# Input and forget gates of a two-way mLSTM mixer: from columns per token to rows along time

## Chip, cores and metric

One Trainium2 chip, one of its cores. The metric is device time of one execution in microseconds (us). The engines named are TensorE (PE, with PEld its weight loads), VectorE (DVE), ScalarE (ACT), GpSimd (POOL) and SyncE (SP), which issues the weight transfers.

## The reference, cut to what matters

Two blocks follow each other on 256 tokens of width 1024 in float32: first a gated DeltaNet layer and an attention layer with feed-forward halves, then a block with adaptive modulation, feed-forward halves and a token mixer. The change is in that mixer. It projects 256 context tokens and 256 latent tokens and runs a stabilised mLSTM over each, forward and backward, with 4 heads of 256. The context run starts from zero and gives the state from which the latent run starts. Its gates are 16 of the projected columns: for each direction an input gate and a forget gate for each of 4 heads.

```python
gate_pre = (gates[0], jax.nn.log_sigmoid(gates[1]), gates[2], jax.nn.log_sigmoid(gates[3]))
# one direction, one chunk; lix: input gates, lfx: log forget gates, along time
b = jnp.cumsum(lfx, axis=-1)
dmat = b[..., :, None] - b[..., None, :] + lix[..., None, :]
inter = b + m[..., None]
m_t = jnp.maximum(inter, jnp.max(jnp.where(lower, dmat, -jnp.inf), axis=-1))
w, a = jnp.exp(dmat - m_t[..., None]), jnp.exp(inter - m_t)
h = num / jnp.maximum(jnp.abs(den), jnp.exp(-m_t))[..., None]
```

So the kernel needs, for 8 pairs of direction and head, a running sum of softplus(-f) along time, a running maximum of (input gate + sum), and exponentials of these, partly as rows along time and partly as columns, one value for each token.

## The kernel before, in words

Nearly all the work is matrix products with weights that stream from HBM in chunks of 1 MB. Each chunk is cut into a high and a low part (`whi` by ACT, line 382; `wlo` by DVE, line 388), and each product is three float32r products: high by high, high by low, low by high. Chunks go through rings of three buffers. `cut_ahead(engine, c)` stands in ACT's and DVE's order after the work on chunk c and cuts chunk c+3; ACT's cut waits until the products of chunk c are done (`used`), DVE's until ACT's is done, the products of a chunk wait for DVE's, and a later transfer into the raw buffer waits for DVE's as well. The order of work on each engine is written out by hand at the end of the file; engines meet by semaphores, and each runs its own list strictly in order.

The stretch around the change runs over segments of the weight stream: `down3` (end of a feed-forward half), `c_k`, `c_v` (context keys and values), `l_k`, `l_v`, `l_q` (latent keys, values, queries), `l_f`, `l_o`. `c_k`, `l_k`, `l_q` have 4 chunks each, with 48 products of 256 moving columns per chunk (line 411, for the first chunk of `l_k` line 472); `c_v`, `l_v` have 4 chunks with 24 products of 512 columns (line 454). `stream_pe(..., more)` calls `more(j)` after the products of chunk j. `conv_act` copies a chunk's result out of PSUM with a bias (`tap_x`, line 1983), applies Silu to the chunk before (line 1975), cuts ahead and then does its own `more(j)`; `conv_dve` does three-tap convolutions (lines 2004 to 2012), cuts ahead and calls `more(j)`. `values_dve` takes the values out of PSUM.

The gates pass (`gates_pe`, products recorded at line 411 on tiles `swh`, `swl`) uses activations as the stationary operand and 16 weight columns as the moving one: 2 token tiles x 8 x 3 = 48 products of 16 columns, once for the context before `c_k` and once for the latent after chunk 1 of `l_k`. `m_gates_dve` and `m_gates_act` form softplus(-f) on columns. `m_rows_pe` (lines 2077 to 2091) makes rows and running sums out of the columns by products with the identity, with all ones and with triangles; `m_rows_dve` copies the rows out and scans for the maximum; `m_rows_act` takes exponentials; `m_cols_pe` (line 2149) turns rows back to columns by products with a 4x4 identity. Then `st_pe` (line 2258) multiplies queries and keys, `cm_pe` (2242, 2244) spreads rows over partitions, `part_pe` forms the outputs. `update_pe`, `update_act`, `update_dve` (lines 2195, 2207, 2214) build the 8 context states: ACT scales keys to `kw`, PE multiplies, DVE copies out. `turn_*` transposes the next input, `rms_*` normalises it: ACT squares, POOL takes the root (line 1932), DVE scales (line 1937). `load_params` issues small parameter transfers on SP's queue between the first weight chunks, ahead of the transfer of `table`, for which `params_pe` waits.

Of the kernel before, what the change touches and what calls it, by code (L numbers as in the profile page):

```python
# [23 lines left out]
P = 128  # L24
# [30 lines left out]
    "m_gate": ("clev0", 4), "m_soft": ("w_ps", 24), "m_log": ("wlev", 24),  # L55
    "m_exp": ("twt_ps", 24), "m_rows_ps": ("invup", 20), "m_rows": ("invtup", 24),
    "m_first": ("row_am", 4), "m_next": ("decl", 16), "m_scan": ("deca", 16), "m_nlast": ("erow", 2),
# [31 lines left out]
def shape_tables():  # L89
# [18 lines left out]
    for h in range(4):  # L108
        sel[h, h] = 1
# [35 lines left out]
def build(nc, A, out):  # L145
# [351 lines left out]
    gate_bias = sm(16)  # L497
# [37 lines left out]
    def load_params(act):  # L535
        for g, members in enumerate(groups):
# [5 lines left out]
        act.dma_start(gate_bias, A["b_in_2"][:, COL_GATES:COL_BR].broadcast_to([P, 16]))\  # L542
           .then_inc(S("params_in"), 16)
        act.dma_start(table[:, P:N_TABLE], A["table"][:, P:N_TABLE]).then_inc(S("tables_in"), 16)
    N_PARAM_DMA = sum(len(m) for m in groups) + 3
# [306 lines left out]
    def small_weight_cut(dve, n):  # L852
        dve.wait_ge(*S("gates_in", 16 * (n + 1)))
        dve.tensor_copy(swh[:, :, :], g_raw[:, :, :]).then_inc(S("gates_cut"), 1)
        dve.wait_ge(*S("gates_cut", 2 * n + 1))
# [3 lines left out]
    def gates_pe(pe, n, out_bank):  # L859


        pe.wait_ge(*S("gates_cut", min(2 * n + 2, 4)))
        if n == 1:
            pe.wait_ge(*S("gate_row", 4))
        for tt in range(TT):
# [5 lines left out]
            last = products(pe, ps[out_bank][:, 16 * tt:16 * tt + 16], pairs)  # L871
# [5 lines left out]
    def gdn_in_pe(pe):  # L877
        pe.wait_ge(*S("act_lo", 4))

        def more(j):  # L880
            if j == 0:
                params_pe(pe)
                gates_pe(pe, 0, 7)
# [1056 lines left out]
    def ffn_banks(tt, h):  # L1940
# [19 lines left out]
    m_state, m_zero, m_nlast = sm(2), sm(2), sm(2)  # L1960
    m_wkc = sm(16).rearrange("p (d t h) -> p d t h", d=2, t=2)
    m_col = sm(48).rearrange("p (d t c h) -> p d t c h", d=2, t=2, c=3)
# [72 lines left out]
    def m_gates_dve(dve, n):  # L2035

        dve.wait_ge(*S("gates_ps", n + 2))
        flat_g = m_gate.rearrange("p t d c h -> p t (d c h)")
# [834 lines left out]
```

## Time and profile before

| | us |
|---|---|
| median of 3 runs | 1801.19 |
| lowest, highest | 1796.42, 1809.6 |
| profiled execution: its own time | 1805.2 |
| its span in the trace | 1803.4 |
| PE busy / DVE / ACT / POOL | 1712.1 / 970.0 / 764.5 / 221.4 |

The span runs from the first to the last instruction of the trace; 1.8 us of the execution's time lie around it. Positions below are us from the span's start. Matrix products are pipelined and their ends are modelled, so the distance from start to start tells their cost. A float32 product (not float32r) shows as two records. The mean granted clock of TensorE over the execution is 0.973 of 2.4 GHz.

### The profile page before, as it was taken

The page shows a single profiled execution, that of the slowest core. Times are in us where ns is not written, and L with a number is a line of the kernel's source. Part 1 is how long each engine was busy: PE and PEld are TensorE (multiplying, and loading weights), DVE is VectorE, ACT ScalarE, POOL GpSimd, SP SyncE. Part 2 cuts the span into 40 slices and gives each one's busy share as a digit, 9 for nine tenths or more (in the row PEclk, how much of TensorE's full clock was granted, in tenths as well). Part 3 has the DMA queues.
Part 4 walks back from the last instruction along what each step waited for, and adds up shares of the span by engine and source line. Part 5 has one row for each costly group of instructions (what it writes and reads, how often), then busy time and mean ns, then how long its engine had stood idle before and what let it go on. Part 6 is the DMA issues. An engine that isn't in the chain of part 4 may idle for free. (4 is left out here: it accounts for less than half of the span.)

```text
span 1803.4 us, 27891 instructions
## 1 busy us (share of the span) xinstructions
PE 1712.1 (95%) x12010; PEld 1567.6 (87%) x12010; DVE 970.0 (54%) x1076; ACT 764.5 (42%) x971; POOL 221.4 (12%) x185
## 2 busy tenths in 40 slices
PE   7999998999897889999999999999999999979998
PEld 7996888998684678988999899989899999969996
DVE  4663247554744464556755565555656354755543
ACT  4453433443344334433444354435455344444442
POOL 0123414000300040001400030002000020030000
PEclk8999999999898999999999999999989899989999
DMA  7554257665467577656765666554434224556652
GB/s 223 164 165 140 71 164 213 184 187 187 163 214 271 169 232 220 181 192 203 189 176 187 187 187 175 177 187 152 133 124 150 74 82 141 167 137 183 171 190 89
DMA packets 329281, 306.56 MB, mean 170 GB/s; under 512 B 12066, under 2 KB 287047, under 8 KB 329031
## 3 DMA queue, kind: packets, MB, share of 16 engines
q1 hardware_dynamic: 324358, 296.20, 53.4%
q10 hardware_dynamic: 4528, 7.54, 1.2%
q8 instruction: 95, 1.56, 0.4%
q0 software_dynamic: 272, 1.05, 0.2%
q14 instruction: 28, 0.22, 0.0%
HBM read 303.70 MB, written 1.05 MB: 169 GB/s over the span
## 5 line engine op out<-in xcount | busy, mean ns | idle before, releaser
L388 DVE TENSOR_TENSOR wlo<-raw,whi 128x2048 fp32r<-128x2048 f32 x247 | 583.7, 2366 | 392.7 <-ACT whi L382 392.5
L411 PE MATMUL ps<-ah,whi 128*128 128x256 f32 x2368 | 679.3, 287 | 7.4 <-DVE wlo L388 7.4
L411 PE MATMUL ps<-al,whi 128*128 128x256 f32 x2368 | 673.2, 284 | 0.0
L411 PE MATMUL ps<-ah,wlo 128*128 128x256 f32 x2368 | 673.0, 284 | 0.0
L382 ACT CAST whi<-raw 128x2048 fp32r<-128x2048 f32 x247 | 469.9, 1904 | 227.4 <-PE ps L435 157.1
L411 PEld LDWEIGHTS ps<-ah,whi 128*128 128x128 f32 x2368 | 457.9, 193 | 12.5 <-issue 9.0
L411 PEld LDWEIGHTS ps<-al,whi 128*128 128x128 f32 x2368 | 457.8, 193 | 1.8 <-issue 1.4
L411 PEld LDWEIGHTS ps<-ah,wlo 128*128 128x128 f32 x2368 | 457.6, 193 | 0.0
L756 ACT ACTIVATE f_sig<-ps 128x256 f32<-128x256 f32 x110 | 42.1, 383 | 372.4 <-PE ps L411 355.9
L435 PE MATMUL ps<-whi,fh 128*128 128x512 f32 x440 | 171.5, 390 | 0.0
L435 PE MATMUL ps<-wlo,fh 128*128 128x512 f32 x440 | 171.2, 389 | 0.0
L435 PE MATMUL ps<-whi,fl 128*128 128x512 f32 x440 | 171.2, 389 | 0.0
L785 DVE TENSOR_TENSOR f_act<-ps,f_sig 128x256 f32<-128x256 f32 x110 | 46.5, 423 | 153.0 <-ACT f_sig L756 152.9
L454 PE MATMUL ps<-whi,ah 128*128 128x512 f32 x256 | 103.1, 403 | 3.1 <-DVE al L616 1.8
L454 PE MATMUL ps<-wlo,ah 128*128 128x512 f32 x256 | 100.9, 394 | 0.0
L454 PE MATMUL ps<-whi,al 128*128 128x512 f32 x256 | 100.7, 393 | 0.0
L435 PEld LDWEIGHTS ps<-whi,fl 128*128 128x128 f32 x440 | 82.6, 188 | 17.1
L435 PEld LDWEIGHTS ps<-wlo,fh 128*128 128x128 f32 x440 | 82.6, 188 | 16.9
L435 PEld LDWEIGHTS ps<-whi,fh 128*128 128x128 f32 x440 | 82.6, 188 | 16.9
L454 PEld LDWEIGHTS ps<-whi,ah 128*128 128x128 f32 x256 | 49.0, 191 | 14.2 <-issue 2.6
L454 PEld LDWEIGHTS ps<-whi,al 128*128 128x128 f32 x256 | 48.8, 191 | 10.5
L454 PEld LDWEIGHTS ps<-wlo,ah 128*128 128x128 f32 x256 | 48.9, 191 | 10.0 <-issue 0.2
(359 smaller groups left out, 1778.0 us busy)
## 6 DMA issues: line engine op xcount, KB each, us to landing
raw<-in_f_w SPq DMA_DIRECT2D x132, 512.0 KB, 4.6
raw<-in_w_a SPq DMA_DIRECT2D x132, 512.0 KB, 4.5
raw<-in_w_ada SPq DMA_DIRECT2D x72, 512.0 KB, 4.6
raw<-in_w_in SPq DMA_DIRECT2D x68, 512.0 KB, 4.6
raw<-in_w_b SPq DMA_DIRECT2D x66, 512.0 KB, 4.5
raw<-in_a_w_in SPq DMA_DIRECT2D x32, 512.0 KB, 5.2
raw<-in_b_w_qkv SPq DMA_DIRECT2D x24, 512.0 KB, 4.8
raw<-in_a_w_out SPq DMA_DIRECT2D x8, 512.0 KB, 3.9
```

What stands on the lines that cost most here:

```text
L382: act.copy(whi[:, c % RING, :], raw[:, r % RING, :]).then_inc(S("hi_ready"), 1)
L388: dve.tensor_tensor(wlo[:, c % RING, :], raw[:, r % RING, :], whi[:, c % RING, :].bitcast(F32), ALU.subtract).then_inc(S("lo_ready"), 1)
L411: last = pe.matmul(out_ap, a, b, start=(i == 0), stop=(i == n - 1))
L435: last = pe.matmul(ps[4 + 2 * tt + h][:, :], x[:, k, cols_], y[:, kk, n], start=(k == 0 and i == 0), stop=(k == KF - 1 and i == 2))
L454: last = pe.matmul(ps[q.bank[first + tt]][:, :], x[:, 4 * half + kk, cols_], y[:, kk, :], start=(half == 0 and kk == 0 and i == 0), stop=( ...
L756: act.activation(f_sig[:, j % RING, :], ps[b][:, 0:T], ACT.Silu).then_inc(S("silu"), 1)
L785: dve.tensor_tensor(f_act[:, j % RING, :], ps[b][:, T:2 * T], f_sig[:, j % RING, :], ALU.mult)\
```

## The change

The gate weights are spread over 100 of 128 stationary columns: POOL zeroes two tiles `gwh`, `gwl` (`gate_weights_pool`), DVE cuts the 16 weight columns into them (`gate_weights_dve`) so that forward and backward input gates fall on rows 0 to 3 and 32 to 35 of the result and forget gates on rows 64 to 67 and 96 to 99. The weights become the stationary operand and the activations the moving one: 8 x 3 = 24 products of 256 columns give rows along time at once (`m_gates_pe`), for the context after chunk 1 of `c_k`, for the latent after chunk 1 of `l_k`. ACT takes them out of PSUM with a bias for each row (`m_gates_act`), DVE forms |f| (`m_size_dve`), ACT applies Exp and Ln one chunk later (`m_soft_act`, each with its table load), DVE forms the running sums by scans and then the running maxima (`m_rows_dve`, one chunk later again). `m_rows_pe` is gone. `m_cols_pe` turns 36 rows at once: 2 products in place of 4 for the context, 6 in place of 12 for the latent, the latter moved from after `l_f` chunk 0 to after `l_q` chunk 1. `m_cols_dve` copies in 2 and 6 instructions in place of 1 and 1. The bias is now loaded by four transfers in place of one, after two DVE memsets, and `sel` holds ones on rows 32 to 35 too.

```diff
+        for d in range(2):
+            for c in range(2):
+                row, at_ = 64 * c + 32 * d, COL_GATES + 8 * d + 4 * c
+                act.dma_start(gate_bias[row:row + 4, :],
+                              A["b_in_2"][0, at_:at_ + 4].rearrange("(h o) -> h o", o=1))\
+                   .then_inc(S("params_in"), 16)
         act.dma_start(table[:, P:N_TABLE], A["table"][:, P:N_TABLE]).then_inc(S("tables_in"), 16)
-    N_PARAM_DMA = sum(len(m) for m in groups) + 3
+    N_PARAM_DMA = sum(len(m) for m in groups) + 6
+    def setup_dve(dve):
+        dve.memset(gate_bias[0:64, :], 0.0).then_inc(S("bias_zero"), 1)
...
     cell = at("cell", 47.125, [P, 2, NH, 2, W1])
-    m_r0, m_cm0, m_a, m_r1, m_s1, m_cm1 = (at(f"m_row{kb}_{i}", kb, [P, 2, T])
-                                           for i, kb in enumerate((74, 76, 39.125, 72, 74, 76)))
+    gwh, gwl = at("gwh", 25.125, [P, KD, P], F32R), at("gwl", 29.125, [P, KD, P], F32R)
+    m_sp, m_s, m_r, m_cm = ([at(f"m_row{n}{kb}", kb, [P, T]) for n, kb in enumerate(kbs)]
+                            for kbs in ((74, 72), (75, 73), (76, 74), (77, 76)))
+    m_a = at("m_a", 77, [P, T])
     w_buf = [at(f"w_buf{kb}", kb, [P, 512]) for kb in (8, 10, 12, 14, 72, 74)]
     m_nq = at("m_nq", 63.25, [P, NH, W1])
-    m_gate = sm(32).rearrange("p (t d c h) -> p t d c h", t=2, d=2, c=2)
-    m_sp, m_mx = (sm(16).rearrange("p (t d h) -> p t d h", t=2, d=2) for _ in range(2))
...
+    def gate_weights_pool(pool):
+        pool.wait_ge(*used("down3", segs["down3"].n - 1))
+        pool.memset(gwh[:, :, :].bitcast(F32), 0.0).then_inc(S("gw_zero"), 1)
+        pool.memset(gwl[:, :, :].bitcast(F32), 0.0).then_inc(S("gw_zero"), 1)
+    def gate_weights_dve(dve):
+        dve.wait_ge(*S("gates_in", 32))
+        dve.wait_ge(*S("gw_zero", 2))
+        w = g_raw[:, :, :].rearrange("p k (d c h) -> p k d c h", d=2, c=2)
+        hi, lo = (g[:, :, :].rearrange("p k (c d r) -> p k d c r", c=2, d=2) for g in (gwh, gwl))
+        for c in range(2):
+            dve.tensor_copy(hi[:, :, :, c, 0:4], w[:, :, :, c, :]).then_inc(S("m_gw"), 1)
+        for c in range(2):
+            dve.wait_ge(*S("m_gw", c + 1))
+            dve.tensor_tensor(lo[:, :, :, c, 0:4], w[:, :, :, c, :], hi[:, :, :, c, 0:4].bitcast(F32), ALU.subtract)\
+               .then_inc(S("m_gw"), 1)
+    def m_gates_pe(pe, n):
+        pe.wait_ge(*S("m_gw", 4))
+        if n == 0:
+            pe.wait_ge(*S("gate_row", 4))
+        pairs = []
+        for k in range(KD):
+            pairs += [(gwh[:, k, 0:100], ah[:, k, :]), (gwh[:, k, 0:100], al[:, k, :]), (gwl[:, k, 0:100], ah[:, k, :])]
+        products(pe, ps[3][0:100, 0:T], pairs).then_inc(S("gates_ps"), 1)
+    def m_gates_act(act, n):
+        act.wait_ge(*S("gates_ps", n + 2))
+        act.activation(m_sp[n][ROWS, :], ps[3][64:100, 0:T], ACT.Identity, bias=gate_bias[64:100, :])\
+           .then_inc(S("m_f"), 1)
+        act.activation(m_r[n][ROWS, :], ps[3][ROWS, 0:T], ACT.Identity, bias=gate_bias[ROWS, :])\
+           .then_inc(S("m_f"), 1)
+    def m_size_dve(dve, n):
+        f, least = m_sp[n][ROWS, :], m_s[n][ROWS, :]
+        dve.wait_ge(*S("m_f", 2 * n + 2))
+        dve.tensor_scalar(least, f, 0.0, None, ALU.min).then_inc(S("m_soft"), 1)
+        dve.wait_ge(*S("m_soft", 3 * n + 1))
+        dve.scalar_tensor_tensor(f, least, -2.0, f, ALU.mult, ALU.add).then_inc(S("m_soft"), 1)
+    def m_soft_act(act, n):
+        f = m_sp[n][ROWS, :]
+        act.wait_ge(*S("m_soft", 3 * n + 2))
+        act.activation(f, f, ACT.Exp, scale=-1.0).then_inc(S("m_exp"), 1)
+        act.wait_ge(*S("m_exp", n + 1))
+        act.activation(f, f, ACT.Ln, bias=1.0).then_inc(S("m_log"), 1)
+    def along(buf, d):
+        a = buf[DIRS[d], :]
+        return a[:, ::-1] if d else a
+    def m_rows_dve(dve, n):
+        sp, cum, r, cm = m_sp[n], m_s[n], m_r[n], m_cm[n]
+        if n == 0:
+            for buf in (m_zero, m_nlast, m_state):
+                dve.memset(buf[ROWS, :], 0.0).then_inc(S("m_zeros"), 1)
         dve.wait_ge(*S("m_log", n + 1))
-        dve.tensor_tensor(m_sp, m_sp, m_mx, ALU.add).then_inc(S("m_soft"), 1)
...
+        dve.tensor_tensor(sp[ROWS, :], sp[ROWS, :], cum[ROWS, :], ALU.subtract).then_inc(S("m_soft"), 1)
+        dve.wait_ge(*S("m_soft", 3 * n + 3))
+        dve.wait_ge(*S("m_zeros", 3))
         for d in range(2):
-            u = tab("uf" if d == 0 else "ub")
...
+            dve.tensor_tensor_scan(along(cum, d), along(sp, d), along(sp, d), m_zero[DIRS[d], :], ALU.add, ALU.max)\
+               .then_inc(S("m_cum"), 1)
+        dve.wait_ge(*S("m_cum", 2 * n + 2))
+        dve.tensor_tensor(r[ROWS, :], r[ROWS, :], cum[ROWS, :], ALU.add).then_inc(S("m_r"), 1)
+        dve.wait_ge(*S("m_r", n + 1))
+        if n:
+            dve.wait_ge(*S("m_next", 2))
         for d in range(2):
-            u = tab("uf" if d == 0 else "ub")
...
+            init = (m_zero, m_state)[n]
+            dve.tensor_tensor_scan(along(cm, d), along(r, d), along(r, d), init[DIRS[d], :], ALU.max, ALU.max)\
+               .then_inc(S("m_scan"), 1)
         dve.wait_ge(*S("m_scan", 2 * n + 2))
         if n == 0:
             for d in range(2):
-                last = cm[0:4, d, (T - 1, 0)[d]:(T, 1)[d]]
-                dve.tensor_scalar(m_nlast[0:4, d:d + 1], last, -1.0, None, ALU.mult).then_inc(S("m_nlast"), 1)
-                dve.tensor_tensor(m_state[0:4, d:d + 1], last, ps[5][0:4, d:d + 1], ALU.subtract)\
-                   .then_inc(S("m_next"), 1)
+                p, t = slice(32 * d, 32 * d + 4), slice((T - 1, 0)[d], (T, 1)[d])
+                dve.tensor_scalar(m_nlast[p, :], cm[p, t], -1.0, None, ALU.mult).then_inc(S("m_nlast"), 1)
+                dve.tensor_tensor(m_state[p, :], cm[p, t], cum[p, t], ALU.subtract).then_inc(S("m_next"), 1)
         else:
-            dve.tensor_tensor(m_s1[0:4, :, :], m_cm1[0:4, :, :], m_s1[0:4, :, :], ALU.subtract)\
-               .then_inc(S("m_mt"), 1)
+            dve.tensor_tensor(cum[ROWS, :], cm[ROWS, :], cum[ROWS, :], ALU.subtract).then_inc(S("m_mt"), 1)
     def m_rows_act(act, n):
         if n == 0:
             act.wait_ge(*S("m_nlast", 2))
-            for d in range(2):
-                act.activation(row(m_r0, d), row(m_r0, d), ACT.Exp, bias=m_nlast[0:4, d:d + 1])\
-                   .then_inc(S("m_wk"), 1)
+            act.activation(m_r[0][ROWS, :], m_r[0][ROWS, :], ACT.Exp, bias=m_nlast[ROWS, :]).then_inc(S("m_wk"), 1)
             return
         act.wait_ge(*S("m_scan", 4))
-        for d in range(2):
-            act.activation(row(m_a, d), row(m_cm1, d), ACT.Exp, scale=-1.0, bias=m_state[0:4, d:d + 1])\
-               .then_inc(S("m_a"), 1)
+        act.activation(m_a[ROWS, :], m_cm[1][ROWS, :], ACT.Exp, scale=-1.0, bias=m_state[ROWS, :])\
+           .then_inc(S("m_a"), 1)
         act.wait_ge(*S("m_mt", 1))
-        act.activation(m_s1[0:4, :, :], m_s1[0:4, :, :], ACT.Exp, scale=-1.0).then_inc(S("m_em"), 1)
+        act.activation(m_s[1][ROWS, :], m_s[1][ROWS, :], ACT.Exp, scale=-1.0).then_inc(S("m_em"), 1)
     def m_cols_pe(pe, n):
         if n == 0:
-            pe.wait_ge(*S("m_wk", 2))
-            out_, kinds = ps[4], [m_r0]
+            pe.wait_ge(*S("m_wk", 1))
+            pe.wait_ge(*S("res_scaled", 8))
+            kinds = [m_r[0]]
         else:
-            pe.wait_ge(*S("m_a", 2))
+            pe.wait_ge(*S("m_a", 1))
             pe.wait_ge(*S("m_em", 1))
-            pe.wait_ge(*evicted("l_q", 3))
-            out_, kinds = ps[1], [m_r1, m_a, m_s1]
-        for d in range(2):
+            pe.wait_ge(*S("cell", 16))
+            kinds = [m_r[1], m_a, m_s[1]]
+        for c, buf in enumerate(kinds):
             for tt in range(TT):
-                for c, buf in enumerate(kinds):
-                    at_ = ((d * 2 + tt) * len(kinds) + c) * 4
-                    last = pe.matmul(out_[:, at_:at_ + 4], buf[0:4, d, tt * P:tt * P + P], ident[0:4, 0:4],
-                                     start=True, stop=True)
+                at_ = 36 * (TT * c + tt)
+                last = pe.matmul(ps[4][:, at_:at_ + 36], buf[ROWS, tt * P:tt * P + P], ident[ROWS, 0:36],
+                                 start=True, stop=True)
         last.then_inc(S("m_cols_ps"), 1)
     def m_cols_dve(dve, n):
         dve.wait_ge(*S("m_cols_ps", n + 1))
-        if n == 0:
...
+        for c in range((1, 3)[n]):
+            dst = m_wkc if n == 0 else m_col[:, c, :, :, :]
+            for d in range(2):
+                src = ps[4][:, 72 * c:72 * c + 72].rearrange("p (t r) -> p t r", t=TT)[:, :, 32 * d:32 * d + 4]
+                dve.tensor_copy(dst[:, :, d, :], src).then_inc(S("m_cols"), 1)
     def k_tok_pe(pe, blocks):
         for b in blocks:
...
@@ -2555,13 +2559,10 @@
         pe.wait_ge(*S("act_lo", 24))
         ffn_pe(pe, 3, gate=1, down_turn=6)
         pe.wait_ge(*S("act_lo", 28))
-        gates_pe(pe, 1, 3)
-        stream_pe(pe, "c_k", ah, al)
-        pe.wait_ge(*S("m_gate", 1))
+        stream_pe(pe, "c_k", ah, al, lambda j: m_gates_pe(pe, 0) if j == 1 else None)
+        pe.wait_ge(*S("m_f", 2))
         def context_rows(j):
-            if j == 0:
-                m_rows_pe(pe, 0)
             if j == 2:
                 m_cols_pe(pe, 0)
                 k_tok_pe(pe, (0, 1))
...
         def keys_and_gates(j):
             if j == 1:
-                gates_pe(pe, 2, 3)
+                m_gates_pe(pe, 1)
             updates({0: 2, 1: 3, 3: 4})(j)
         stream_pe(pe, "l_k", ah, al, keys_and_gates, turn=7)
-        pe.wait_ge(*S("m_gate", 2))
+        pe.wait_ge(*S("m_f", 4))
         stream_pe(pe, "l_v", ah, al, updates({0: 5, 1: 6, 2: 7}))
-        stream_pe(pe, "l_q", ah, al, lambda j: m_rows_pe(pe, 1) if j == 0 else None)
+        stream_pe(pe, "l_q", ah, al, lambda j: m_cols_pe(pe, 1) if j == 1 else None)
         stream_pe(pe, "l_f", ah, al, only=[0])
-        m_cols_pe(pe, 1)
...
         res_act(act, segs["down3"])
-        m_gates_act(act, 0)
-        conv_act(act, "c_k", kt, lambda j: rms_act(act, 3, x0, "res", 3) if j == 2 else None)
+        def context_gates(j):
+            if j == 1:
+                m_gates_act(act, 0)
+            if j == 2:
+                m_soft_act(act, 0)
+                rms_act(act, 3, x0, "res", 3)
+        conv_act(act, "c_k", kt, context_gates)
         q = segs["c_v"]
...
             if j == 1:
                 m_gates_act(act, 1)
             else:
+                if j == 2:
+                    m_soft_act(act, 1)
                 update_act(act, {0: 3, 2: 4, 3: 5}[j])
         conv_act(act, "l_k", kt, keys_and_gates)
...
-        conv_act(act, "l_q", qt, lambda j: m_rows_act(act, 1) if j == 2 else None)
+        conv_act(act, "l_q", qt, lambda j: m_rows_act(act, 1) if j == 0 else None)
...
         res_dve(dve, 0)
         ffn_dve(dve, 3, up_work=lambda e, j: rms_dve(e, 2, x1) if j == UP_AT else None, down_work=lambda e: turn_dve(e, 6, mod_scale(1)))
-        m_gates_dve(dve, 0)
+        gate_weights_dve(dve)
         mask_dve(dve)
         res_dve(dve, 1)
-        conv_dve(dve, "c_k", lambda j: rms_dve(dve, 3, x0) if j == 2 else None)
+        def context_gates_dve(j):
+            if j == 1:
+                m_size_dve(dve, 0)
+            if j == 2:
+                rms_dve(dve, 3, x0)
+            if j == 3:
+                m_rows_dve(dve, 0)
+        conv_dve(dve, "c_k", context_gates_dve)
         def context_rows_dve(j):
-            if j == 0:
...
         def cells_and_gates(j):
             if j == 1:
-                m_gates_dve(dve, 1)
+                m_size_dve(dve, 1)
             if j:
                 update_dve(dve, j + 1)
+            if j == 3:
+                m_rows_dve(dve, 1)
         conv_dve(dve, "l_k", cells_and_gates)
         values_dve(dve, "l_v", lambda j: update_dve(dve, 5 + j) if j < 3 else None)
-        conv_dve(dve, "l_q", lambda j: m_rows_dve(dve, 1) if j == 1 else None)
+        conv_dve(dve, "l_q", lambda j: m_cols_dve(dve, 1) if j == 2 else None)
...
         gate_rows_pool(pool, 1)
         rms_pool(pool, 2)
         turn_pool(pool, 6, mod_shift(1))
+        gate_weights_pool(pool)
         res_pool(pool, 1, x0)
```

## Rows read from the trace of the kernel before

**Rows 1.** Page, busy time of each engine, share of the span, instructions.

```profile
PE 1712.1 (95%) x12010; PEld 1567.6 (87%) x12010; DVE 970.0 (54%) x1076; ACT 764.5 (42%) x971; POOL 221.4 (12%) x185
```

**Rows 2.** Waits of PE from 1185 to 1440: total, times, longest.

```profile
PE ps L472 <- DVE al L616: 1.9, 1, 1.9
```

**Rows 3.** Timeline of PE, context gates and `c_k`: start, duration, instruction.

```profile
1227.64 0.17 PE L411 MATMUL ps<-swh,ah 128*128 128x16 f32 x1
...
1234.56 0.56 PE L411 MATMUL ps<-ah,whi 128*128 128x256 f32 x1
...
1238.05 0.28 PE L411 MATMUL ps<-al,whi 128*128 128x256 f32 x1
```

**Rows 4.** Timeline of PE, latent gates, updates and chunk 2 of `l_k`.

```profile
1307.19 0.17 PE L411 MATMUL ps<-swh,ah 128*128 128x16 f32 x1
...
1315.07 3.77 PE L2195 MATMUL ps<-v_aug,kw 128*128 128x257 f32 x8
1318.28 0.78 PE L411 MATMUL ps<-ah,whi 128*128 128x256 f32 x1
...
1319.91 0.28 PE L411 MATMUL ps<-ah,whi 128*128 128x256 f32 x1
...
1324.94 0.28 PE L411 MATMUL ps<-ah,whi 128*128 128x256 f32 x1
...
1330.70 1.89 PE L2195 MATMUL ps<-v_aug,kw 128*128 128x257 f32 x8
1332.24 0.58 PE L454 MATMUL ps<-whi,ah 128*128 128x512 f32 x1
```

**Rows 5.** Windows: length, busy PE, PEld, DVE, ACT, POOL, granted clock, DMA.

```profile
1232.00:1234.00 2.00, 2.00 (x11) 2.00 (x11) 0.12 (x1) 1.39 (x3) 1.66 (x6) 0.50 0.38 52
```

**Rows 6.** Timeline of PE, first instruction of each rows pass and its successor.

```profile
1264.71 0.38 PE L2077 MATMUL ps<-table,small 128*4 128x128 f32 x2
...
1267.16 0.50 PE L454 MATMUL ps<-whi,ah 128*128 128x512 f32 x1
...
1365.37 0.38 PE L2077 MATMUL ps<-table,small 128*4 128x128 f32 x2
...
1368.95 0.39 PE L411 MATMUL ps<-ah,whi 128*128 128x256 f32 x1
```

**Rows 7.** Timeline of PE, latent columns and the two query-key passes with their successors.

```profile
1392.17 0.38 PE L2149 MATMUL ps<-table,m_row 4*128 4x4 f32 x2
...
1394.94 5.46 PE L2258 MATMUL ps<-qt,kt 128*128 128x128 f32 x32
1400.15 0.48 PE L2242 MATMUL ps<-negr,identr 128*128 128x512 f32 x1
...
1422.34 3.74 PE L2258 MATMUL ps<-qt,kt 128*128 128x128 f32 x32
1425.83 0.48 PE L2242 MATMUL ps<-negr,identr 128*128 128x512 f32 x1
```

**Rows 8.** Timeline of ACT: update after `l_k` chunk 3; a switch to Exp.

```profile
1333.95 0.91 ACT L2207 ACTIVATE kw<-k_tok,small 128x256 f32<-128x256 f32 x2
...
1382.01 1.90 ACT L382 CAST whi<-raw 128x2048 fp32r<-128x2048 f32 x1
1383.93 1.28 ACT L2131 ACT_TABLE_LOAD   x1
1385.22 0.91 ACT L2131 ACTIVATE m_row39.125_2_94<-m_row,small 4x256 f32<-4x256 f32 x2
```

**Rows 9.** Timeline of DVE, chunks 2 and 3 of `c_k`; what it waited for in brackets.

```profile
1259.88 0.75 DVE L1937 TENSOR_SCALAR xn<-x,small 128x1024 f32<-128x1024 f32 x1 [0.72 <-POOL small L1932]
...
1264.25 2.28 DVE L388 TENSOR_TENSOR wlo<-raw,whi 128x2048 fp32r<-128x2048 f32 x1
```

**Rows 10.** All scans on the row tiles: duration in ns, minimum, median, maximum.

```profile
L2110 DVE TENSOR_TENSOR_SCAN m_row<-m_row,small x4: 712/724/737, 1269.9 to 1382.4; 4x256 f32<-4x256 f32 x4
```

**Rows 11.** Timeline of SP's queue, issue of the one bias transfer.

```profile
16.31 0.43 SPq L542 DMA_DIRECT2D small<-in_b_in  x1
```

More of the change, by code:

```diff
@@ L108, in shape_tables @@
     for h in range(4):
-        sel[h, h] = 1
+        sel[h, h] = sel[32 + h, h] = 1
     t["sel"] = sel.reshape(P, 4 * P)
@@ L870, in gates_pe @@
                           (al[:, k, c], swh[:, k, :])]
-            last = products(pe, ps[out_bank][:, 16 * tt:16 * tt + 16], pairs)
+            last = products(pe, ps[7][:, 16 * tt:16 * tt + 16], pairs)
         last.then_inc(S("gates_ps"), 1)
@@ L882, in more @@
                 params_pe(pe)
-                gates_pe(pe, 0, 7)
+                gates_pe(pe)
             if j == 2:
@@ L2051, in m_gates_act @@
-    def m_gates_act(act, n):
-        act.wait_ge(*S("m_soft", 4 * n + 3))
-        act.activation(m_sp, m_sp, ACT.Exp, scale=-1.0).then_inc(S("m_exp"), 1)
-        act.wait_ge(*S("m_exp", n + 1))
-        act.activation(m_sp, m_sp, ACT.Ln, bias=1.0).then_inc(S("m_log"), 1)
-    def front(d):
-        return d
-    def row(buf, d):
-        return buf[0:4, d, :]
-    def m_rows_pe(pe, n):
-        pe.wait_ge(*S("m_soft", 4 * n + 4))
-        if n == 0:
-            pe.wait_ge(*S("res_scaled", 8))
-        else:
-            pe.wait_ge(*S("cell", 16))
-        for d in range(2):
-            u = tab("uf" if d == 0 else "ub")
-            for tt in range(TT):
-                o = ps[4][0:4, T * d + P * tt:T * d + P * tt + P]
-                pe.matmul(o, m_gate[:, tt, d, 0, :], ident, start=(d == tt == 0), stop=False)
-                if tt != front(d):
-                    pe.matmul(o, m_sp[:, front(d), d, :], ones, start=False, stop=False)
-                pe.matmul(o, m_sp[:, tt, d, :], u, start=False, stop=(d == tt == 1))
-        for d in range(2):
-            u = tab("uf" if d == 0 else "ub")
-            for tt in range(TT):
-                if n == 0:
-                    last = pe.matmul(ps[5][0:4, d:d + 1], m_sp[:, tt, d, :], ones[:, 0:1],
-                                     start=(tt == 0), stop=(tt == 1))
-                else:
-                    o = ps[5][0:4, T * d + P * tt:T * d + P * tt + P]
-                    if tt != front(d):
-                        pe.matmul(o, m_sp[:, front(d), d, :], ones, start=(d == tt == 0), stop=False)
-                    last = pe.matmul(o, m_sp[:, tt, d, :], u, start=(d == tt == 0), stop=(d == tt == 1))
-        last.then_inc(S("m_rows_ps"), 1)
@@ L2094, in m_rows_dve @@
[L2094 to L2110 removed]
+    ROWS = slice(0, 36)
@@ L2243, in cm_pe @@
             for h in range(NH):
-                last = pe.matmul(bank(b, NH)[:, h, :], tab("sel", 4)[0:4, h, :], m_cm1[0:4, d, tile],
+                last = pe.matmul(bank(b, NH)[:, h, :], tab("sel", 4)[32 * d:32 * d + 4, h, :], m_cm[1][32 * d:32 * d + 4, tile],
                                  start=(i == 2 and h == 0), stop=(h == NH - 1))
@@ L2311, in part_act @@
             wait_from(act, *S("hout", i - 3))
-            act.activation(m_nq[:, h, :], ps[part_banks(h)[0]][:, 0:W1], ACT.Copy, scale=m_col[:, d, t, 1, h:h + 1])\
+            act.activation(m_nq[:, h, :], ps[part_banks(h)[0]][:, 0:W1], ACT.Copy, scale=m_col[:, 1, t, d, h:h + 1])\
                .then_inc(S("nq"), 1)
@@ L2726, in _ @@
     def _(dve):
+        setup_dve(dve)
         turn_dve(dve, 0)
         start_cuts(dve)
-        small_weight_cut(dve, 0)
+        small_weight_cut(dve)
         gdn_in_dve(dve)
```

86 lines of the change are left out of this document (23 added, 63 removed).

## The prediction

> **What bounds the kernel now.** I read the page's busy times first [rows 1]: PE is busy 95% of the span, no other engine over 54%. The share says little about one stage, so next come the waits of PE in the stretch that the change touches: in 255 us there is one wait, of 1.9 us [rows 2], before the transposed input of `l_k`, and it follows PE's own transposes. So in this stretch PE's list is the critical path, and every us that leaves PE's list or its starts comes off the time, unless ACT or DVE fall behind. The third view is the timeline of PE, read start to start, because recorded durations overlap. In the fast state a product of 256 columns costs (1324.94 - 1319.91) / 42 = 0.120 us [rows 4], a chunk of 48 such products 5.76 us. The fourth is the windows: in the middle of the first gates pass the granted clock is 0.50, the lower of TensorE's levels (1.2 GHz), though PE sat idle nowhere [rows 5]. What PE did before the fall was products of 16 columns, and it stayed at the low level into the chunk behind them.
>
> **Parts that leave or change PE's list.**
>
> (a) Context gates. From the first product of the pass to the first of `c_k` it is 1234.56 - 1227.64 = 6.92 us [rows 3]. The next 16 products take 1238.05 - 1234.56 = 3.49 us, 0.218 each, against 16 x 0.120 = 1.92: a tail of 1.57. In their place come 24 products of 256 columns: 2.88 us at 0.120, at most 5.2 at the slow 0.218. The nearest row is the stream's own product, the same form but for 28 stationary columns, so I take 2.88. Gain 6.92 + 1.57 - 2.88 = 5.61.
>
> (b) Latent gates. 1315.07 - 1307.19 = 7.88 us for the pass. The update behind it takes 1318.28 - 1315.07 = 3.21, where an ordinary one takes 1332.24 - 1330.70 = 1.54: 1.67 more. Six slow products take 1.63 instead of 0.72, of which I leave 0.2 to the handover: 0.7 more [rows 4]. Gain 7.88 + 1.67 + 0.7 - 2.88 = 7.37.
>
> (c) The products for rows go: 1267.16 - 1264.71 = 2.45 for the context, 1368.95 - 1365.37 = 3.58 for the latent [rows 6]. Gain 6.03.
>
> (d) Products for columns. The latent pass takes 1394.94 - 1392.17 = 2.77 us for 24 records, 0.115 each [rows 7]. Six float32 products leave 12 records, 1.38 us, among full chunks of `l_q`; for the context 4 records of 8 go, 0.46. Gain 1.39 + 0.46 = 1.85. A 36-row product could cost up to the 0.163 of a slow query-key record (5.21 / 32, below); that is 0.8 us less for the 16, and nothing makes it cheaper than 0.115.
>
> (e) The query-key pass that followed those columns products takes 1400.15 - 1394.94 = 5.21 us, the second one, with the same records and no columns products ahead of it, 1425.83 - 1422.34 = 3.49 [rows 7]. With the small products gone from its front I expect 3.49. Gain 1.72, bounds 0 and 3.2 (a later slow stretch might go too, or the same one move behind it).
>
> Gross: 5.61 + 7.37 + 6.03 + 1.85 + 1.72 = 22.6 us.
>
> Of the first two and the last, 1.57 + 1.67 + 0.7 + 1.72 = 5.7 us are the slow clock's and not the products'. The Trainium skill, in "TensorE: Matmul & The Clock Gate", section "HAM oscillation", puts the fall down to idle gaps of the array. By that rule PE, which has no idle gap here, would not owe its slow stretches to these products, and they would stay. The rows show the fall without a gap, so I hold to the rows; the rule's outcome is the first rival.
>
> **Parts that other engines now owe PE.**
>
> (f) ACT before the update after `l_k` chunk 3. PE finishes chunk 3 at 1330.70 and ACT starts that chunk's own extra work at 1333.95 [rows 4, 8]: 3.25 us for copying out, Silu and the cut. In the new order chunk 2's extra work is Exp and Ln on 256 columns, each behind a table switch, and then the two `kw` for update 4. A switch takes 1.28, an activation of 256 columns 0.91 / 2 = 0.45 to 0.5 [rows 8]: 2 x 1.28 + 2 x 0.5 = 3.6 us. If PE ends chunk 2 at X, the first `kw` is there at X + 3.25 + 3.6 + 0.45 = X + 7.3; PE wants it after chunk 3, at X + 5.76. A new stall of 1.55 us, 1.6 with the handover. Queued behind on ACT is the copy of chunk 3 out of its bank, which `l_v` needs: it ends 0.5 before that.
>
> The rows show no more than the load itself: cut until 1383.91, load at 1383.93, Exp at 1385.22 [rows 8]. The Trainium skill, "ScalarE: Activation LUTs", section "What ACT_TABLE_LOAD costs", adds a drain of about 1.38 us to each. By it the stall would be 1.6 + 2.8 = 4.4 and the sum below 17.4 instead of 20.2; the rows decide.
>
> (g) DVE's cuts for `c_v`. Before, chunk 2 of `c_k` ended at 1238.05 + 128 x 0.120 = 1253.4; DVE's first scaling of the next input, which needs ACT's squares and POOL's root, began at 1259.88, 6.5 later, and the list from there to the cut took 4.37 and the cut 2.28 [rows 3, 9]. Now chunk 2 ends at 1227.64 + 3 x 5.76 + 2.88 = 1247.8, and (f)'s 3.6 us stand ahead of the squares: 1247.8 + 6.5 + 3.6 + 4.37 + 2.28 = 1264.5. PE wants this chunk after four of `c_k` (1253.56) and two of `c_v`, of (1264.71 - 1253.4 - 5.76) = 5.5 each [rows 3, 6]: 1264.6. Just met. Then DVE runs the new rows block: four scans at 0.72 [rows 10] are 2.9, two whole-tile steps and seven small ones some 1.4 (my estimate from half a scan each for the former), 4.3 in all; bounds 2.5 and 7, since an adding scan has no row of its own. The cut behind it is done at 1264.5 + 4.3 + 2.3 = 1271.1. PE wants it after a third chunk (1270.1), the columns products (0.46) and the key transposes behind them, so at 1270.6 or later. I put 0.1 us of stall; by the upper bound it is 2.7.
>
> (h) Start. Three more transfers are issued on SP ahead of `table` and of the fourth weight chunk; one takes 0.43 and a gap of 0.04 [rows 11], 1.4 in all. `params_pe` waits for `table`, the whole queue stands behind. Bounds 0 (table lands while chunk 0 is multiplied) and 1.4; I take 0.7.
>
> Covered, and therefore nothing: POOL's zeroing and DVE's cutting of the gate weights come 11 us before their first product, and the cut queued behind them on DVE serves a chunk three places on; should that cover go, DVE's delay shows there one for one. ACT's Exps for the latent columns, now behind `l_q` chunk 0 (end Y): 3.25 less a Silu of 0.5, then 1.28 + 2 x 0.5 ends at Y + 5.0, and PE asks at Y + 5.76, so 0.7 us of cover. The latent rows block stands behind the cut for `l_v` chunk 2 and ahead of the one for chunk 3, which PE needs three chunks and three updates later. Six column copies on DVE lie beside chunks 2 and 3 of `l_q`. After the stretch PE's waits follow PE's own transposes, so the shift should travel to the end.
>
> Net: 22.6 - 1.6 - 0.1 - 0.7 = 20.2 us. The profiled execution took 1805.2 us, 1.8 more than its span: 1785.0. It lay 4.0 above the median of three, so I forecast 1801.2 - 20.2 = 1781.0.
>
> **Rivals.**
>
> 1. The slow clock stays. For it: nothing here shows 100-column weights at work, and the low level needs no idle gap. Against: streams of 256-column products keep the high level all through. Then the 5.7 us stay and 48 products cost 0.218: 4.7 more. 20.2 - 10.4 = 9.8: 1791. Chance 0.12.
> 2. ACT and DVE fall behind. (g) has no slack, (f) is a stall already, and each us on DVE's rows block or ACT's switches is passed on. For it: two switches in series in front of squares, POOL, DVE and a cut. Against: all else keeps 0.5 us or more. With the upper bound of (g), 2.7, that of (h), 1.4, and 3 more in (f): 20.2 - 2.6 - 0.7 - 3 = 13.9: 1787. Chance 0.20.
> 3. It doesn't do what it says for the whole: the gain is made by 1400 and given back at a later wait that doesn't follow PE. Nothing in the stretch shows one, but I have not followed every wait to 1803. 1801. Chance 0.06.
> 4. Slower. One mechanism: scans with addition, or on 36 partitions, run ten times slower than the row of 0.72. The context block holds four, 26 us more in front of a cut without cover; the latent block four, 26 less some 10 of cover. 20.2 - 26 - 16 gives 1823. It turns slower than before once a scan costs over some 4.5 us. The scans measured, one of each pair reversed in time, lie within 25 ns of each other, so 0.04.
>
> **How the numbers follow.** Forecast 0.58, rivals 0.12, 0.20, 0.06, 0.04. About 1% (18 us) is what a measurement of this kernel can tell from no change; three runs spread over 13 us. The forecast lies only 2 us beyond that bound; rivals 1 to 3 lie within it. So faster 0.58, same 0.38, slower 0.04. Range: downward all of (e)'s upper bound, no stalls in (f) to (h) and some of the spread of medians, 1781 - 1.5 - 2.4 - 4 = 1773; upward rivals 2 and 1, 1792. Rivals 3 and 4 stay out.
>
> **What would show it.** Right: PE's granted clock at 1.00 through both gates passes, 24 products in 2.9 us, no product for rows, a wait of PE for ACT's `kw` of 1.6 us after `l_k` chunk 3, the first query-key pass at 3.5 us. Wrong in (a), (b): clock at 0.50 behind the new products. Wrong in (g): PE waiting for `wlo` in `c_v`. Wrong in (f): a wait above 3 us. The prediction fails if ACT's new place delays more than one cut, or if a slow stretch appears that before did not have.

## The result and the profile after

The changed kernel takes 1781.2 us (median of 4 runs, 1780.0 to 1786.1), the kernel before 1804.1 beside it (4 runs, 1796.4 to 1809.6): ratio 0.988, 95% interval 0.984 to 0.993. A second series gave 1782.7 against 1805.1 and 0.988 again. That is 1.2% faster, 22 to 23 us where 20.2 were forecast; the forecast time, 1781.0, was met to 0.2 us by luck: the difference was forecast 2 to 3 us too small, and the median of before that it started from, 1801.2, lay 3 to 4 us below the 1804 to 1805 of more runs. The profiled execution took 1782.3, 1.9 more than its span.

The page of the changed kernel first, span and busy times, which answer to [rows 1]:

```profile
span 1780.4 us, 27662 instructions
PE 1689.6 (95%) x11886; PEld 1547.3 (87%) x11886; DVE 975.9 (55%) x1087; ACT 766.2 (43%) x973; POOL 222.4 (12%) x187
```

The span is 23.0 us shorter, PE is busy 22.5 us less, and DVE only 6 us more. PE's waits from 1160 to 1440, as in [rows 2]:

```profile
PE ps L472 <- DVE al L626: 1.9, 1, 1.9
PE ps L2199 <- ACT kw L2211: 1.4, 1, 1.4
```

The old wait is there, and one new one, (f)'s. Timeline of PE: the context gates from their first to their last record and the stream's product behind them (against [rows 3]); the first record of the latent gates and the update behind them; the update after chunk 3 of `l_k` (against [rows 4]); the latent columns (one of four records, and their successor); and both query-key passes with their successors (against [rows 7]):

```profile
1241.80 0.28 PE L411 MATMUL ps<-ah,gwh 128*100 128x256 f32 x1
...
1244.49 0.28 PE L411 MATMUL ps<-ah,gwl 128*100 128x256 f32 x1
1244.60 0.28 PE L411 MATMUL ps<-ah,whi 128*128 128x256 f32 x1
...
1301.06 0.28 PE L411 MATMUL ps<-ah,gwh 128*100 128x256 f32 x1
...
1303.86 1.90 PE L2199 MATMUL ps<-v_aug,kw 128*128 128x257 f32 x8
...
1318.70 1.97 PE L2199 MATMUL ps<-v_aug,kw 128*128 128x257 f32 x8 [1.44 <-ACT kw L2211]
...
1359.21 0.63 PE L2155 MATMUL ps<-table,m_row 36*128 36x36 f32 x4
...
1360.66 0.39 PE L411 MATMUL ps<-ah,whi 128*128 128x256 f32 x1
...
1378.02 3.74 PE L2262 MATMUL ps<-qt,kt 128*128 128x128 f32 x32
1381.52 0.48 PE L2246 MATMUL ps<-negr,identr 128*128 128x512 f32 x1
...
1403.69 3.74 PE L2262 MATMUL ps<-qt,kt 128*128 128x128 f32 x32
1407.18 0.48 PE L2246 MATMUL ps<-negr,identr 128*128 128x512 f32 x1
```

Read start to start: 24 gates products take 2.80 us, 0.117 each, both times; 12 records for columns 1.45; the first query-key pass 3.50 where it was 5.21. The windows (length, busy PE, granted clock, DMA) show the high level, 2.4 GHz, in the middle of both gates passes, where [rows 5] had 0.50:

```profile
1242.00:1244.00 2.00, 2.00 (x19) 1.00 0.00 0
1302.00:1304.00 2.00, 2.00 (x19) 1.00 0.80 309
```

What lay behind the one new wait, from ACT's timeline (against [rows 8]):

```profile
1314.71 1.28 ACT L2092 ACT_TABLE_LOAD   x1
1316.01 0.42 ACT L2092 ACTIVATE m_row<-m_row 36x256 f32<-36x256 f32 x1
1316.45 1.28 ACT L2094 ACT_TABLE_LOAD   x1
1317.74 0.42 ACT L2094 ACTIVATE m_row<-m_row 36x256 f32<-36x256 f32 x1
1318.06 0.89 ACT L2211 ACTIVATE kw<-k_tok,small 128x256 f32<-128x256 f32 x2
1318.86 0.81 ACT L1989 ACTIVATE tap_x<-ps,cols 128x256 f32<-128x256 f32 x2
```

The second load begins 0.44 after the first Exp began: nothing but the 1.28 of the load itself stands between two activations. And DVE's new rows block of the context, between the cuts for chunks 2 and 3 of `c_v` (against [rows 9, 10]):

```profile
1263.74 2.29 DVE L388 TENSOR_TENSOR wlo<-raw,whi 128x2048 fp32r<-128x2048 f32 x1
...
1266.47 1.51 DVE L2111 TENSOR_TENSOR_SCAN m_row<-m_row,small 32x256 f32<-32x256 f32 x2
1268.01 0.42 DVE L2114 TENSOR_TENSOR m_row<-m_row,m_row 36x256 f32<-36x256 f32 x1
1268.46 1.51 DVE L2120 TENSOR_TENSOR_SCAN m_row<-m_row,small 32x256 f32<-32x256 f32 x2
...
1270.49 2.29 DVE L388 TENSOR_TENSOR wlo<-raw,whi 128x2048 fp32r<-128x2048 f32 x1
```

The block takes 4.5 us, a scan 0.74 by its own record (1.51 for two), whether it adds or takes the maximum, and PE does not wait for the cut.

**The stretch in marks.** I cut PE's timeline at instructions that both kernels have: end of the FFN (A), first transpose for `l_k` (B), first query-key pass (C), its end (D), second pass, its end (E), first product of the stream behind the outputs that follow the second pass (F). A is a position, the other columns are lengths. Each kernel was profiled twice:

| | A | A to B | B to C | C to D | E to F |
|---|---|---|---|---|---|
| before | 1227.6 | 58.89 | 108.41 | 5.21 | 14.06 |
| before, second profile | 1229.1 | 60.49 | 108.34 | 5.22 | 10.75 |
| after | 1230.3 | 50.11 | 97.62 | 3.50 | 10.41 |
| after, second profile | 1227.6 | 50.10 | 97.62 | 3.49 | 13.71 |

B to C and C to D repeat within 0.1 us here, which points to the list of instructions; the variants below show that B to C can also grow by 1.5 by a slow stretch that comes and goes. A to B differs by 1.6 between the profiles of before. D to E, not in the table, is 25.7 in three of the four and 24.2 in the second profile of before. E to F differs by 3.3 between two profiles of the same kernel, in either kernel: the fall of the clock there comes and goes. Had I compared the first pair alone, I would have booked 3.65 us to the change that it did not bring.

### The profile page after: what moved, and what is told of

The parts are those of the page before. It is cut to its first block and busy times, and to the rows that moved or that the text cites. A ratio compares the mean times of both kernels' runs of the same rounds, so it can differ in the third digit from the quotient of the medians.

```text
span 1780.4 us, 27662 instructions
## 1 busy us (share of the span) xinstructions
PE 1689.6 (95%) x11886; PEld 1547.3 (87%) x11886; DVE 975.9 (55%) x1087; ACT 766.2 (43%) x973; POOL 222.4 (12%) x187
## 5 line engine op out<-in xcount | busy, mean ns | idle before, releaser
L454 PEld LDWEIGHTS ps<-whi,al 128*128 128x128 f32 x256 | 48.6, 190 | 10.4
```

The costliest lines, as they stand in the source:

```text
L454: last = pe.matmul(ps[q.bank[first + tt]][:, :], x[:, 4 * half + kk, cols_], y[:, kk, :], start=(half == 0 and kk == 0 and i == 0), stop=( ...
```

## The experiments

**1. Is it the clock, and is PE's list the path?** Two kernels answer this. The first is the kernel before, which keeps its 48 products of each gates pass, but each reads the 16 columns 16 times over, so that it has 256 (the output and the copy behind it are widened to match):

```diff
+            r = 16 if n else 1
+            hi, lo = (w.unsqueeze(2).to_broadcast([P, KD, r, 16]) for w in (swh[:, :, :], swl[:, :, :]))
...
-                pairs += [(ah[:, k, c], swh[:, k, :]), (ah[:, k, c], swl[:, k, :]),
-                          (al[:, k, c], swh[:, k, :])]
+                pairs += [(ah[:, k, c], hi[:, k]), (ah[:, k, c], lo[:, k]), (al[:, k, c], hi[:, k])]
...
```

> The kernel before, with one edit: in the context and latent gates passes the moving operand of each of the 48 products repeats its 16 columns 16 times, 256 columns in all; the sums read are the same. Theory (the low clock comes from the products of 16 columns, not from idle gaps): both passes run at the high level, 48 x 0.120 = 5.8 us each in place of 6.9 + 1.6 and of 7.9 + 1.7 + 0.7, so although PE does 16 times the columns the time falls by 2.7 + 4.5 = 7.2 us. Rival (the slow stretch belongs to the place and stays): 48 x 0.218 = 10.5 us each, 6 us slower than before. Rival (a product's cost is its columns alone): 5.8 against the 6.9 and 7.9 of the passes, but with the tails still there, 3.2 us faster.

In the second the changed kernel runs each new gates pass twice:

```diff
+        products(pe, ps[3][0:100, 0:T], pairs)
         products(pe, ps[3][0:100, 0:T], pairs).then_inc(S("gates_ps"), 1)
```

> The changed kernel with each of its two new gates passes done twice, 48 products of 256 columns in place of 24. Theory (PE's list is the time here, the new products keep the clock): 2 x 24 x 0.120 = 5.8 us more than the changed kernel, about 16 us less than before. Rival (other engines set the time of this stretch by now): under 2 us more. Rival (products with 100 stationary columns lower the clock once there are enough of them): over 10 us more.

The first took 1798.4 (10 runs) against 1804.5 (14), ratio 0.997, interval 0.995 to 0.999. Sixteen times the columns took less time: 6.1 us less between the medians where 7.2 were expected. Its PE timeline, first product of each pass and what follows it, and three windows:

```profile
1224.89 0.28 PE L411 MATMUL ps<-swh,ah 128*128 128x256 f32 x1
...
1230.74 0.28 PE L411 MATMUL ps<-ah,whi 128*128 128x256 f32 x1
...
1309.14 1.90 PE L2197 MATMUL ps<-v_aug,kw 128*128 128x257 f32 x8
```

```profile
1226.00:1228.00 2.00, 2.00 (x19) 1.00 1.03 391
1304.00:1306.00 2.00, 2.00 (x19) 1.00 0.87 299
1290.00:1292.00 2.00, 2.00 (x12) 0.50 0.00 0
```

The pass takes 5.85 instead of 6.92 and leaves no tail: A to B is 2.63 shorter than in the first profile of before, as expected (2.7), and 4.2 shorter than in the second, where the pass took 7.93. B to C is 2.95 shorter, not 4.5: a new stretch at 0.50 came up at 1290, behind the old 1.9 us wait, and cost 1.5. The second kernel took 1785.7 (5 runs, ratio to before 0.991, 0.988 to 0.994). Its last windows in the two passes:

```profile
1247.00:1249.00 2.00, 2.00 (x20) 1.00 0.10 14
1309.00:1311.00 2.00, 2.00 (x19) 1.00 0.00 0
```

A to B grew by 2.80, B to C by 2.79, and neither C to D nor E to F moved against the first profile of the changed kernel: each us on PE's list is a us of the time there, and 48 products of 100 stationary columns in a row hold the high level as well. Over the whole kernel the medians differ by less than these 5.6 us, by 3.0 to 4.5 against the two series of the changed kernel.

**2. Does the first query-key pass owe its 1.7 us to the columns products ahead of it?** The six new products were moved back to straight ahead of the pass, into bank 1:

```diff
-        stream_pe(pe, "l_q", ah, al, lambda j: m_cols_pe(pe, 1) if j == 1 else None)
+        stream_pe(pe, "l_q", ah, al)
         stream_pe(pe, "l_f", ah, al, only=[0])
+        m_cols_pe(pe, 1)
...
```

> The changed kernel with the latent columns products put back to their old place, between chunk 0 of l_f and the first query-key pass, with bank 1 as their target as before; still 12 records. To be read in the trace. Theory of the prediction's step (e) (small products ahead of the query-key pass bring the clock down in it): the first query-key pass takes about 5.2 us again in place of 3.5, and the slow stretch near the second pass comes back too. Rival (it was the chance of where the slow stretch fell): the pass stays at 3.5 us.

One run: 1788.7. The pass was slow (5.12), but it also had a gap of 4.1 us in front, since it waited for the columns' eviction, so the run can't tell the products from the gap. In the next kernel it waits for the context's columns alone:

```diff
-            pe.wait_ge(*S("m_cols", 8))
+            pe.wait_ge(*S("m_cols", 2))
```

> The changed kernel with the six products for columns moved back to where they stood, straight ahead of the first query-key pass, in a bank of their own, and the pass no longer waiting for their eviction: the idle gap of 4.1 us in the run before this one is gone, and the products alone are left. If it was the gap that brought the clock down there: pass 3.5, second pass with its decay products and the part behind it 3.5, 3.55, 6.86 as in the changed kernel, total within 1 us of it. If short products ahead of the pass do it (as the rows and columns did before): pass 5.1, some 1.6 us, and perhaps the second fall too (3.7 us).

And with 24 products of 4 moving columns instead of the six of 36:

```diff
+                for lo, hi in ((0, 36),) if n == 0 else ((0, 4), (32, 36)) * 2:
+                    last = pe.matmul(ps[(4, 1)[n]][:, at_ + lo:at_ + hi], buf[ROWS, tt * P:tt * P + P],
+                                     ident[ROWS, lo:hi], start=True, stop=True)
```

> The changed kernel with the products for columns straight ahead of the first query-key pass, as in the run without the gap, but 24 products of 4 moving columns in place of 6 of 36 (each twice; the last writes stand): as near as it can be to what stood there in the kernel before. The products cost 2.8 in place of about 1.4. If products of few columns ahead of the pass are what brought the clock down in the kernel before, the pass takes 5.1 instead of 3.6 here; if not, it stays 3.5 to 3.6 and the cause lies further ahead (the rows products and the slow stretches that they leave).

They took 1785.3 and 1791.8 (one run each). The query-key pass in PE's timeline, in the three kernels in this order, in the third with the first row of the products ahead of it:

```profile
1379.11 5.36 PE L2262 MATMUL ps<-qt,kt 128*128 128x128 f32 x32 [4.08 <-issue]
```

```profile
1377.29 3.84 PE L2262 MATMUL ps<-qt,kt 128*128 128x128 f32 x32
```

```profile
1373.58 1.95 PE L2156 MATMUL ps<-table,m_row 36*128 36x4 f32 x16
...
1379.33 6.75 PE L2263 MATMUL ps<-qt,kt 128*128 128x128 f32 x32
```

and the windows of the third, PE busy throughout:

```profile
1376.00:1378.00 2.00, 2.00 (x20) 1.00 1.02 356
1378.00:1380.00 2.00, 2.00 (x13) 0.66 0.20 30
1380.00:1382.00 2.00, 2.00 (x11) 0.50 0.97 263
```

So two different things bring the clock down: a gap (first kernel, 0.50 in its window behind it) and products of few columns without any gap (third kernel). Behind the six products of 36 columns, 1.45 us, the pass took 3.6 (second kernel). They cost PE the same as among `l_q`; B to C came out 1.4 longer by one stretch of low clock behind the 1.9 us wait. That bears out (e), with two reserves. The 24 products left 48 records and took 5.75 us, where [rows 7] had 24 records in 2.8, so the dose was larger than the original (the pass behind took 6.5, not 5.2). And each of the two kernels has one trace; but the pass took 5.2 in all three traces with the old columns products ahead of it (two of before, one of the widened kernel) and 3.5 in all seven that have the new ones among `l_q`.

**3. How much of it belongs to the list?** Both kernels profiled again, unaltered.

> The changed kernel once more, unaltered, as the bound for what one profile can say. If the fall of the clock behind the second query-key pass (3.7 us in the profile of the kernel before, none in that of the changed one) belongs to the instruction list, this profile has none either: second pass 3.49, its decay products 3.55, the part behind them 6.86. If it comes and goes from run to run, one of the three may be longer. The stretch from the end of the FFN to the first query-key pass stays 147.7 within 0.3. Ratio to before 0.988.

> The kernel before once more, unaltered, with a profile. If the slow first query-key pass (5.21) belongs to its instruction list, it is 5.2 again; if it comes and goes as the fall behind the second pass does in the changed kernel (there in one profile, not in the other), this profile may show 3.5. From the end of the FFN to the first query-key pass: 167.3 within 1.5 if the list sets it, since one slow stretch more or less costs 1.5 in the profiles so far.

1782.7 (4 runs) and 1802.9 (one). The first pass is 5.2 again in before; the marks are in the table above. The fall behind the second pass, missing in the first profile of the changed kernel, is in its second (windows as above):

```profile
1406.00:1408.00 2.00, 2.00 (x16) 0.84 0.27 41
1408.00:1410.00 2.00, 2.00 (x7) 0.50 1.04 364
1410.00:1412.00 2.00, 2.00 (x6) 0.50 0.36 119
```

and in the second profile of before it is missing. So the change did not remove it.

**4. How much slack has (g)?** Four more scans in the context rows block:

```diff
+        if n == 0:
+            for i in range(4):
+                dve.wait_ge(*S("m_more", i)) if i else None
+                dve.tensor_tensor_scan(sp[ROWS, :], r[ROWS, :], r[ROWS, :], m_zero[ROWS, :], ALU.max, ALU.max)\
+                   .then_inc(S("m_more"), 1)
```

> The changed kernel with four more scans of 256 elements in the context rows block on DVE, 4 x 0.74 us, results unused. To be read in the trace. Theory of step (g): the block had 1.2 to 1.5 us of cover in the changed kernel's trace, so PE now waits about 1.8 us in all before the columns products and chunk 3 of c_v. Rival (DVE's work here is hidden anyway): no wait of PE in c_v.

One run: 1786.3. The added scans took 3.08 us in all. PE's waits from 1240 to 1440:

```profile
PE ps L472 <- DVE al L626: 1.9, 1, 1.9
PE ps L2204 <- ACT kw L2216: 1.4, 1, 1.4
PE ps L2160 <- ACT m_row L2139: 1.3, 1, 1.3
PE ps L454 <- DVE wlo L388: 0.2, 1, 0.2
```

Two new ones, 1.5 us in all, so the changed kernel had 1.6 us of slack; the prediction had counted on none. The first is put down to ACT, but what is new is DVE's delay ahead of the columns. A to B grew by 3.5: behind the wait the granted clock fell to 0.50 (1278 to 1280), and that cost another 1.9, more than the waits.

**5. The two things left: the pass at the start and the wait for `kw`.** First, the 48 products of 16 columns of the first gates pass, at 24 us, which the change left alone, widened to 256 by the edit of experiment 1, and the copy behind it reads the first 16 of each:

```diff
-        dve.tensor_copy(ba, ps[7][:, 0:32].rearrange("p (t c) -> p t c", t=2)).then_inc(S("ba"), 1)
+        dve.tensor_copy(ba, ps[7][:, :].rearrange("p (t c) -> p t c", t=2)[:, :, 0:16]).then_inc(S("ba"), 1)
```

> The changed kernel, with the 48 products of the first pass of gates, at the start of the kernel, made 256 moving columns wide instead of 16 (each column of the weights read 16 times, so that the work is 16-fold). Theory 1 (products of few columns leave the engine at the lower clock, for themselves and for what comes next): the pass falls from 7.5 to the 5.8 of the same width elsewhere, and the slow stretch behind it (2.4 us lost) goes: about 4 us in all. Theory 2 (the start is bound by the transfers of the first weights and by other engines, so that what TensorE gains there becomes a wait): 0, with an idle stretch behind the pass in its place. Theory 3 (the clock doesn't react): the pass costs 11.7 at the lower clock, 4 us slower.

Second, on ACT, the copy ahead of the Exp and Ln:

```diff
+                update_act(act, {0: 3, 2: 4, 3: 5}[j])
                 if j == 2:
                     m_soft_act(act, 1)
-                update_act(act, {0: 3, 2: 4, 3: 5}[j])
```

> The changed kernel with one edit, on ScalarE: the fifth scaled copy of the keys ahead of the Exp and Ln of the latent gates. Theory 1: TensorE's wait of 1.44 for it goes, and nothing comes in its place: end of the FFN to the first query-key pass 146.3 in place of 147.7. Theory 2: the wait moves to the next product that needs ScalarE, the first chunk of l_v behind the eviction that now stands behind the table loads, 0.8 as in the run with both edits: 147.1.

And both together:

> The changed kernel with two edits: the first pass of gates 256 columns wide as in the run beside this one, and on ScalarE the fifth scaled copy of the keys issued ahead of the two Exp and two Ln of the latent gates, which the changed kernel puts in front of it and for which TensorE waits 1.44 us. If both add: 1.4 + 4 = 5.4 us below the changed kernel, a ratio to before near 0.985. If the start is bound elsewhere: 1.4 alone. If the wait for the copy only moves to the next consumer of ScalarE's gates (the running sums on VectorE, then the columns on TensorE): the 1.4 comes back as a wait for the decay rows.

The wide pass: windows of the changed kernel, then of this one.

```profile
28.00:30.00 2.00, 2.00 (x11) 0.50 1.10 350
36.00:38.00 2.00, 2.00 (x13) 0.60 0.00 1
```

```profile
28.00:30.00 2.00, 2.00 (x19) 1.00 1.11 351
36.00:38.00 2.00, 2.00 (x19) 1.00 0.12 43
```

The pass takes 5.9 (25.08 to 30.99) instead of 7.5 (24.35 to 31.87), and by 46 us PE is 3.5 and 2.4 ahead of the two profiles of the changed kernel, of the 4 expected, with no wait in its place. In the whole time, 1780.7 (4 runs, 1778.9 to 1786.2) against 1782.7, it isn't clear of the spread: between 500 and 650 us the stretches of low clock lay otherwise, and at A (1228.4) the lead over the second profile had become a lag of 0.8.

The reordered copy (one run, 1779.9): the wait of 1.44 is gone and PE's timeline has another,

```profile
1318.10 0.47 PE L454 MATMUL ps<-whi,ah 128*128 128x512 f32 x1 [0.82 <-ACT tap_x L1989]
```

`l_v`'s first chunk, for the bank that ACT now empties after the two table loads. B to C is 96.98, 0.64 shorter: theory 2.

Both together: 1776.6 (5 runs, 1772.7 to 1779.5), ratio to before 0.985, 0.982 to 0.987, against 1781.8 to 1784.1 for the changed kernel in the same series; the runs don't overlap. 6.1 us between the medians where 5.4 were expected. Against the second profile of the changed kernel the trace accounts for 3.0 at the start and 0.6 for the copy. It also has no fall behind either query-key pass (1.5 and 3.3 us less), which by experiment 3 need not be the edits' doing, and one of 1.5 behind the 1.9 us wait for `al`, so that B to C comes out at 98.5. It is the fastest version here.

## Why the prediction was right

The mechanism held: PE's list was the path, and the products of few columns cost more than their own records. The sizes, term by term:

(a), (b): 2.80 per pass instead of 2.88. Rival 1 is out by the windows and the doubled pass. Of the gain, 2.6 in (a) (4.2 by the second profile of before) and up to 4.4 in (b) are the clock's, as the widened kernel shows for the same number of products; halving the products gives 3.0 each time. The Trainium skill's rule on idle gaps ("TensorE: Matmul & The Clock Gate", "HAM oscillation") describes the 4.1 us gap of experiment 2. It doesn't describe the falls behind products of 4 and 16 columns, where PE was busy in every window; there the measurement decides, and the change was worth more than by the rule.

(c), (d): not measured alone. By steps (a), (c), (d) and (g), A to B should shrink by 5.61 + 2.45 + 0.46 - 0.1 = 8.4; it shrank by 8.8 in the first pair of profiles and by 10.4 in the second, where the slow stretch of before was longer. By (b), (c), (d) and (f), B to C by 7.37 + 3.58 + 1.39 - 1.6 = 10.7; it was 10.8 in one pair of profiles and 10.7 in the other. Errors could cancel only inside such a sum. The 12 records cost 1.45 instead of 1.38.

(e): 5.21 to 3.50, as forecast, and the cause holds with the reserves given. Its upper bound of 3.2, the later slow stretch, isn't the change's.

(f): 1.44 instead of 1.6, at the place named. The 1.38 of drain at each load that the Trainium skill states ("ScalarE: Activation LUTs", "What ACT_TABLE_LOAD costs") does not show; by it the wait would have been 4.4.

(g): no stall, and 1.6 us of slack where I had 0.1 of stall: cut for chunk 2 done at 1266.0, 35.7 after A, where I forecast 1264.5, 36.9 after the A of before. The block took 4.5 instead of 4.3. Rival 2 did not happen, but four more scans brought it about. Rival 4 falls with the scan at 0.74. The new gate weights were ready at 1235.2, 6.6 us ahead of their first product where the prediction had 11; PE did not wait for them.

(h): 0 instead of 0.7. SP issues the four transfers in 1.34, and PE's `params_pe` starts at 24.03, right behind chunk 0, without a wait. That is later than in before (23.47, second profile 23.64), because chunk 0 itself took 7.7 instead of 7.2; it took 8.6 in the widened kernel of experiment 1, which has the old list there.

Rival 3: from F to the end of the kernel nothing is given back. That stretch took 363.5 and 363.0 in before, 362.8 and 363.2 in the changed kernel. A to D, which holds all of (a) to (g), shrank by 8.8 + 10.8 + 1.7 = 21.3 in the first pair of profiles and by 10.4 + 10.7 + 1.7 = 22.8 in the second, of the 22 to 23 us of the medians; the difference is within what the clock adds or takes from run to run.

## What to carry to other kernels

Look in the windows for the clock where PE is busy without a gap but its products have few moving columns: such a pass costs more than its own records, because what comes behind starts at the low level. Put the few columns on the stationary side, or, if the shape is fixed, repeat them: sixteen times the columns in two passes took 0.3% off this kernel. Before booking a few us to a change, profile both kernels at least twice and compare the marks: what doesn't repeat is not the change's. Two profiles are a small sample: a slow stretch of 1.5 us behind the 1.9 us wait came up in 4 of 13 traces.

## Not expected of the hardware

- Stretches of low clock come up at the same place in one execution of a list and not in the next: behind the second query-key pass in 1 of 2 profiles of either kernel, 3.3 us each; behind the 1.9 us wait for `al` in neither profile of the changed kernel, but in two variants of it with the same list up to there (the first two of experiment 2), and in the widened kernel of experiment 1 and the last of experiment 5. The Trainium skill, "TensorE: Matmul & The Clock Gate", section "Part 1: The HAM clock gate", says of a kernel's start that the same kernel can meet the gate differently from run to run; these traces show the same in mid-kernel.
- DVE's first two steps of the convolution took 3.8 us in the changed kernel beside POOL's additions, and 0.73 for the next chunk. Timeline of DVE, then of POOL:

```profile
1238.57 3.82 DVE L2010 TENSOR_SCALAR tap_y<-tap_x,cols 128x256 f32<-128x256 f32 x2
...
1246.10 0.73 DVE L2010 TENSOR_SCALAR tap_y<-tap_x,cols 128x256 f32<-128x256 f32 x2
```

```profile
1237.42 4.83 POOL L1903 TENSOR_TENSOR x<-x,xn 128x1024 f32<-128x1024 f32 x2 [0.52 <-DVE xn L1910]
```

  DVE had room there. The Trainium skill, "SBUF — State Buffer", section "SBUF: two separate sides", describes a port pair that POOL's operations and some of DVE's lock for a whole instruction, which would fit. In before, where the step overlapped only the last 0.8 us of POOL's additions, it took 1.26. No run tests it.
